# The rounded products read and write their 512 columns in pieces of 8, in turn from the two halves

## The chip, the cores and the metric

The kernel runs on one core of one Trainium2 chip. The metric is the device time of one execution in microseconds (us); the time before is the median of 3 runs.

## What is computed

The reference runs a chain of transformer layers in float32 on a sequence of 512 tokens of width 1024. The first block mixes four heads of a gated delta network with four heads of retention and follows with a convolutional gated MLP of width 2816. Two further layers, with a dilated window attention and a differential attention, each have an MLP of width 4096 with a squared ReLU. Norms stand between them. By far the most arithmetic is in the dense projections:

```python
proj = jnp.einsum('bsd,dc->bsc', n, w_in[l])
...
hdn = jnp.einsum('bsd,df->bsf', x, w_up)
...
return jnp.einsum('bsf,fd->bsd', jax.nn.silu(g) * u, w_down)
...
qkv = xn @ w_qkv
...
h = jax.nn.relu(xn @ w_in)
return (h * h) @ w_out
```

## The kernel before, in words

Activations lie transposed: a tile has 128 features on the partitions and all 512 tokens as its columns, so every projection is a sum over 128-row tiles of "weights (128 x 128, stationary) times activations (128 x 512, moving)" into one PSUM bank of 128 x 512 float32.

TensorE is fed with rounded float32 (`F32R`). To keep the accuracy, each operand is split into a rounded high part and a rounded rest: the activations into `n_hi` and `n_lo` (or `ff_hi` and `ff_lo`, `b_parts`), the weights into `w_hi` and `w_lo`. A product is then three matmuls into the same bank, high x high, high x low and low x high, lines 839, 840 and 841 of the helper `products`. Every dense projection of every layer goes through this helper. Other matmuls (transposes, attention scores and values, column sums) have lines of their own. Most take plain float32 operands; the helper for the scores of the second attention (L1477) and two lines for small gates (L1505, L1506, with 16 and 8 weight columns) use rounded ones but do not go through `products`.

Weights come in units of 256 output columns by 1024 rows (1 MB): SP issues the DMA into `raw`, ScalarE rounds it into `w_hi` (L1569, `split_hi`), VectorE computes `w_lo = raw - w_hi` (L1574, `split_lo`), and TensorE does the unit's 48 matmuls: 2 tiles of 128 output columns, 8 tiles of the sum, 3 matmuls each. `raw`, `w_hi` and `w_lo` have two buffers each. ScalarE waits for `w_used`, which TensorE counts up at the end of a unit, before it overwrites a buffer; TensorE waits for `lo_ready`. The results go to `proj_bank`, four banks in two groups of two; ScalarE or VectorE reads a bank once its last product has signalled, and signals `bank_free`.

The order of the work on TensorE is written out by hand: `project` runs over the units, and in the two attention layers a table of steps puts the attention's matmuls between the products (`layer_a_tensor`, `layer_b_tensor`). In SBUF two small unused tensors, `pad` (384 bytes a partition) at the front and `moving_pad` (160 bytes) ahead of the activations, set where the later tensors start. A tile of activations is 2048 bytes a partition, and the columns 0 to 255 of it are its first 1024 bytes.

Of the kernel before, what the change touches and what calls it, by code (L numbers as in the profile page):

```python
# [203 lines left out]
def build(nc, t, out):  # L204
# [7 lines left out]
    def sb(name, shape, dt=F32):  # L212
        return ctx.enter_context(nc.sbuf_tensor(name, shape, dt))
# [6 lines left out]
    with ctx:  # L220
# [4 lines left out]
        w_hi = sb("w_hi", [P, 2, UNIT], F32R)  # L225
        w_lo = sb("w_lo", [P, 2, UNIT], F32R)
# [606 lines left out]
            norm_pool(pool, 7)  # L833


        def products(b, j, tile, k, hi, lo, start, final):

            cols = slice(k * GC + tile * P, k * GC + tile * P + P)
            nc.tensor.matmul(b[:, :], w_hi[:, j % 2, cols], hi, start=start, stop=False)  # L839
            nc.tensor.matmul(b[:, :], w_hi[:, j % 2, cols], lo, start=False, stop=False)  # L840
            return nc.tensor.matmul(b[:, :], w_lo[:, j % 2, cols], hi, start=False, stop=final)  # L841

        def project(pe, ph, hi, lo, tiles_ready=None, norm=None, pairs_ready=None, order=range(KD), between=None, begun=0):

# [3 lines left out]
            def three(j, g, tile, k, src, start, final):  # L848
                return products(proj_bank[2 * g + tile], j, tile, k, hi[src], lo[src], start, final)
# [351 lines left out]
        def output(pe, ph, unit, k, hi, lo, ready):  # L1201

            if k == 0:
                pe.wait_ge(bank_free, ph.g0 + unit + 1)
                pe.wait_ge(lo_ready, ph.u0 + unit + 1)
            pe.wait_ge(ready[0], ready[1] + k + 1)
            for tile in range(2):
                ins = products(proj_bank[2 * unit + tile], unit, tile, k, hi[k], lo[k], k == 0, k == KD - 1)
                if k == KD - 1:
                    ins.then_inc(w_used if tile else tile0_ready, 1)  # L1210
# [26 lines left out]
        def layer_a_tensor(pe):  # L1237

            ph = p_qkvs[0]
            for step in range(A_STEPS):  # L1240
                u, tile, k = step // (2 * KD), step // KD % 2, step % KD
                attention_a_parts(pe, step)
                if step % (2 * KD) == 0:
                    pe.wait_ge(lo_ready, ph.u0 + u + 1)
                if u == 0:
                    k, tile = divmod(step, 2)
                    if step == 0:
                        pe.wait_ge(bank_free, ph.g0 + 1)
                    if tile == 0:
                        pe.wait_ge(norm_lo, KD * SPLIT[2] + k + 1)  # L1250
                elif k == 0:
                    if u <= 2:
                        pe.wait_ge(bank_free, ph.g0 + u + 1)
                    elif tile == 0:
                        pe.wait_ge(at("a_tile0"), u)
                    else:
                        pe.wait_ge(bank_free, ph.g0 + u + 2)
                ins = products(proj_bank[2 * (u == 1) + tile], u, tile, k, N_HI[k], N_LO[k], k == 0, k == KD - 1)
                if k == KD - 1:
                    ins.then_inc(w_used if tile else tile0_ready, 1)  # L1260
                if u == 1 and (tile, k) == (0, 7):
                    two_sums_of(pe)
                elif u == 1 and (tile, k) == (1, 1):
                    norm_spread(pe, 2)
# [1673 lines left out]
```

## Time and profile before

| what | value |
|---|---|
| median of 3 runs | 1899.64 us (1899.3 to 1900.44) |
| the profiled execution, its own time | 1901.63 us |
| its span, first to last instruction | 1899.8 us |
| mean granted TensorE clock | 0.997 of full speed |
| TensorE matmuls busy | 1880.5 us (99%), 9573 instructions |
| weight loads busy (they overlap the matmuls) | 1523.8 us (80%) |
| VectorE, ScalarE, GpSimd busy | 1052.5 us (55%), 770.4 us (41%), 78.6 us (4%) |

The profiled execution is 2.0 us longer than the median, and 1.8 us of it lie outside the span. Matmuls are pipelined, so one lasts longer in the profile (about 390 ns) than the time until the next starts; the time per matmul is read from the distances between starts or ends, not from its duration. A float32 matmul that is not rounded stands in the profile as two rows of instructions, each with a weight load of its own.

### The profile page before, as it was taken

How to read it: one execution, taken by the hardware profiler on the slowest of the kernel's cores; microseconds unless marked ns; L12 is line 12 of the kernel's file. 1: busy time of each engine (PE TensorE's matmuls, PEld its weight loads, DVE VectorE, ACT ScalarE, POOL GpSimd, SP SyncE). 2: the span in 40 equal slices, each digit the busy share in tenths (PEclk: the TensorE clock that was granted, in tenths of full speed). 3: DMA queues.
4: the chain of work that ended last, by engine and by line, in shares of the span. 5: the costliest groups of instructions: out<-in, count | busy, mean ns of one | idle time of the engine just before them, and what ended most of it. 6: DMA issues, size and time to landing. Idle time of an engine off the chain costs nothing.

```text
span 1899.8 us, 25523 instructions
## 1 busy us (share of the span) xinstructions
PE 1880.5 (99%) x9573; PEld 1523.8 (80%) x9573; DVE 1052.5 (55%) x1458; ACT 770.4 (41%) x967; POOL 78.6 (4%) x77
## 2 busy tenths in 40 slices
PE   8999999999999999999999999999999999999998
PEld 6778888888888788878888888887676788888887
DVE  7746855677367676566543244247778554323423
ACT  5472343555234344454432133136556543212412
POOL 0010001000000010000100000020000010000001
PEclk9999999999999999999999999999999999999999
DMA  6223122232332252212322322342322133223231
GB/s 238 89 87 116 47 68 67 89 103 73 111 108 83 70 158 83 89 53 83 106 93 89 111 89 92 107 130 86 106 84 87 36 99 110 89 93 106 88 103 53
DMA packets 146483, 178.92 MB, mean 94 GB/s; under 512 B 3549, under 2 KB 140381, under 8 KB 143968
## 3 DMA queue, kind: packets, MB, share of 16 engines
q1 hardware_dynamic: 143008, 160.44, 25.9%
q0 software_dynamic: 3104, 17.10, 2.8%
q8 instruction: 54, 0.88, 0.2%
q10 hardware_dynamic: 288, 0.26, 0.0%
q14 instruction: 29, 0.24, 0.0%
HBM read 173.48 MB, written 2.20 MB: 92 GB/s over the span
## 4 chain that ended last, share of the span: by engine, by line
PE 93%; DVE 4%; ACT 1%; issue 1%; DMA 0%; DVEq 0%; ACTq 0%
PE bank L839 28%; PE bank L841 27%; PE bank L840 27%; PE bank L960 2%; PE bank L1495 2%; PE bank L1477 1%; DVE w_lo L1574 1%; PE bank L966 1%; PE bank L1296 1%; PE bank L954 1%; ACT w_hi L1569 1%; PE bank L1349 1%; PE bank L1053 0%; PE bank L1018 0%; PE bank L1061 0%
## 5 line engine op out<-in xcount | busy, mean ns | idle before, releaser
L839 PE MATMUL bank<-n_hi,w_hi 128*128 128x512 f32 x1504 | 605.3, 402 | 7.6 <-DVE w_lo L1590 6.7
L1569 ACT ACTIVATE w_hi<-raw 128x2048 fp32r<-128x2048 f32 x152 | 291.4, 1917 | 732.2 <-PE bank L841 730.0
L841 PE MATMUL bank<-n_hi,w_lo 128*128 128x512 f32 x1504 | 587.5, 391 | 0.0
L840 PE MATMUL bank<-n_lo,w_hi 128*128 128x512 f32 x1504 | 587.4, 391 | 0.0
L1574 DVE TENSOR_TENSOR w_lo<-raw,w_hi 128x2048 fp32r<-128x2048 f32 x152 | 349.2, 2298 | 275.3 <-ACT w_hi L1569 273.4
L839 PEld LDWEIGHTS bank<-n_hi,w_hi 128*128 128x128 f32 x1504 | 283.3, 188 | 77.8 <-issue 20.7
L841 PEld LDWEIGHTS bank<-n_hi,w_lo 128*128 128x128 f32 x1504 | 283.3, 188 | 60.1
L840 PEld LDWEIGHTS bank<-n_lo,w_hi 128*128 128x128 f32 x1504 | 283.6, 189 | 59.7 <-issue 5.0
L840 PE MATMUL bank<-ff_lo,w_hi 128*128 128x512 f32 x848 | 330.0, 389 | 0.0
L839 PE MATMUL bank<-ff_hi,w_hi 128*128 128x512 f32 x784 | 306.0, 390 | 1.3 <-DVE w_lo L1574 1.3
L841 PE MATMUL bank<-ff_hi,w_lo 128*128 128x512 f32 x784 | 305.1, 389 | 0.0
L840 PEld LDWEIGHTS bank<-ff_lo,w_hi 128*128 128x128 f32 x848 | 159.2, 188 | 33.0 <-issue 0.5
L839 PEld LDWEIGHTS bank<-ff_hi,w_hi 128*128 128x128 f32 x784 | 147.2, 188 | 32.5 <-DVE w_lo L1574 1.7
L841 PEld LDWEIGHTS bank<-ff_hi,w_lo 128*128 128x128 f32 x784 | 147.2, 188 | 30.9
L2523 DVE SCALAR_TENSOR_TENSOR scratch<-bank,rstd 128x512 f32<-128x512 f32 x64 | 44.3, 692 | 133.5 <-PE bank L841 124.8
L2508 DVE TENSOR_TENSOR hT<-hT,bank 128x512 f32<-128x512 f32 (+1 forms) x70 | 48.1, 687 | 125.9 <-PE bank L841 123.1
L2290 DVE SCALAR_TENSOR_TENSOR scratch<-scratch,ffn_w 128x511 f32<-128x511 f32 x88 | 66.1, 751 | 16.8 <-DVE scratch L2290 6.0
L2164 ACT ACTIVATE scratch<-scratch,b_small 128x512 f32<-128x512 f32 x64 | 46.3, 724 | 39.8 <-DVE b_small L2763 38.4
L2760 DVE CUSTOM_DVE_ANT_0 scratch<-bank,b_bias 128x512 f32<-128x512 f32 x64 | 44.3, 691 | 23.4 <-PE bank L1477 19.3
L778 POOL TENSOR_TENSOR scratch<-scratch 128x1024 f32<-128x1024 f32 x5 | 13.5, 2709 | 977.0 <-ACT scratch L1667 977.0
L2278 DVE TENSOR_TENSOR scratch<-bank,rstd 128x512 f32<-128x512 f32 x44 | 30.4, 692 | 24.2 <-PE bank L841 16.8
L2530 DVE TENSOR_TENSOR ff_lo<-scratch,ff_hi 128x1024 f32 x32 | 39.2, 1226 | 8.1 <-ACT ff_hi L2037 7.6
(347 smaller groups left out, 1564.2 us busy)
## 6 DMA issues: line engine op xcount, KB each, us to landing
raw<-in_mlp_w_in SPq DMA_DIRECT2D x32, 1024.0 KB, 5.3
raw<-in_mlp_w_out SPq DMA_DIRECT2D x32, 1024.0 KB, 4.9
raw<-in_w_up SPq DMA_DIRECT2D x22, 1024.0 KB, 4.9
raw<-in_w_units SPq DMA_DIRECT2D x14, 1024.0 KB, 4.8
raw<-in_a_w_qkv SPq DMA_DIRECT2D x12, 1024.0 KB, 5.0
raw<-in_b_w_qkv SPq DMA_DIRECT2D x12, 1024.0 KB, 5.0
b_bias<-bias_table POOLq DMA_DIRECT2D x16, 448.0 KB, 4.4
raw<-in_w_down SPq DMA_DIRECT2D x8, 768.0 KB, 4.5
```

What stands on the lines that cost most here:

```text
L839: nc.tensor.matmul(b[:, :], w_hi[:, j % 2, cols], hi, start=start, stop=False)
L840: nc.tensor.matmul(b[:, :], w_hi[:, j % 2, cols], lo, start=False, stop=False)
L841: return nc.tensor.matmul(b[:, :], w_lo[:, j % 2, cols], hi, start=False, stop=final)
L960: ins = nc.tensor.transpose(b[:, i * P:(i + 1) * P], src(i), ident)
L1569: act.activation(w_hi[:, s, :], raw[:, s, :], ACT.Copy).then_inc(hi_ready, 1)
L1574: dve.tensor_tensor(w_lo[:, s, :], raw[:, s, :], w_hi[:, s, :].bitcast(F32), ALU.subtract).then_inc(lo_ready, 1)
L2164: done(act, act.activation(e, e, ACT.Exp, bias=b_small[:, 8 + 2 * (n % 4) + j:9 + 2 * (n % 4) + j], accum_out=b_small[:, 16 + 2 * (n % 4) ...
L2290: ins = dve.scalar_tensor_tensor(y, taken[:, n, 0:SEQ - back], w, y, ALU.mult, ALU.add)
L2508: ins = dve.tensor_tensor(h, h, b[:, :].unsqueeze(1), ALU.add)
L2523: ins = dve.scalar_tensor_tensor(scratch[:, 2 * g + tile, :], b[:, :], 0.0, rstd[:, :], ALU.max, ALU.mult)
L2530: done(dve, dve.tensor_tensor(ff_lo[:, bass.ds(it * 4 + 2 * g, 2), :], scratch[:, 2 * g:2 * g + 2, :], ff_hi[:, bass.ds(it * 4 + 2 * g, 2) ...
L2760: ring_done(dve, dve.tensor_tensor_reduce(b_s[:, n % 4, j, :], b[:, :], b_bias[:, h % 2, j, i * P:i * P + SEQ], 1.0, -FAR, ALU.add, ALU.ma ...
```

## The change

```diff
+        def woven(at_cols):
+            return at_cols.rearrange("p (h l e) -> p l h e", h=2, e=8)
+
         def products(b, j, tile, k, hi, lo, start, final):
 
             cols = slice(k * GC + tile * P, k * GC + tile * P + P)
-            nc.tensor.matmul(b[:, :], w_hi[:, j % 2, cols], hi, start=start, stop=False)
-            nc.tensor.matmul(b[:, :], w_hi[:, j % 2, cols], lo, start=False, stop=False)
-            return nc.tensor.matmul(b[:, :], w_lo[:, j % 2, cols], hi, start=False, stop=final)
+            out, hi, lo = woven(b[:, :]), woven(hi), woven(lo)
+            nc.tensor.matmul(out, w_hi[:, j % 2, cols], hi, start=start, stop=False)
+            nc.tensor.matmul(out, w_hi[:, j % 2, cols], lo, start=False, stop=False)
+            return nc.tensor.matmul(out, w_lo[:, j % 2, cols], hi, start=False, stop=final)
```

`woven` is another way of walking over the same 512 columns: 8 columns from column 0, 8 from column 256, 8 from column 8, 8 from column 264, and so on, 64 pieces in all, each 32 bytes long, with 1024 bytes between neighbours. The moving operand and the PSUM bank are both walked in this way, so each result lands in the column where it was before. The stationary operand, the number of matmuls, their order on TensorE and every wait stay as they are, and no instruction of another engine changes. In the built program a product's shape reads 128x32x2x8 where it read 128x512. The three lines become 843, 844 and 845.

## Rows read from the trace of the kernel before

**Rows 1.** The page: busy times, granted clock by slice, and the chain that ended last
```profile
PE 1880.5 (99%) x9573; PEld 1523.8 (80%) x9573; DVE 1052.5 (55%) x1458; ACT 770.4 (41%) x967; POOL 78.6 (4%) x77
...
PEclk9999999999999999999999999999999999999999
...
PE 93%; DVE 4%; ACT 1%; issue 1%; DMA 0%; DVEq 0%; ACTq 0%
PE bank L839 28%; PE bank L841 27%; PE bank L840 27%; PE bank L960 2%; PE bank L1495 2%; PE bank L1477 1%; DVE w_lo L1574 1%; PE bank L966 1%; PE bank L1296 1%; PE bank L954 1%; ACT w_hi L1569 1%; PE bank L1349 1%; PE bank L1053 0%; PE bank L1018 0%; PE bank L1061 0%
```

**Rows 2.** One line, L839: duration in ns minimum/median/maximum, first and last start, forms
```profile
L839 PE MATMUL bank<-n_hi,w_hi x1504: 387/389/802, 6.7 to 1800.1; 128*128 128x512 f32 x188
...
L839 PE MATMUL bank<-ff_hi,w_hi x784: 387/389/504, 283.6 to 1887.1; 128*128 128x512 f32 x196
...
L839 PE MATMUL bank<-b_parts,w_hi x64: 389/389/795, 1477.5 to 1537.6; 128*128 128x512 f32 x64
...
L839 PE MATMUL bank<-ff_lo,w_hi x32: 389/389/389, 298.2 to 330.2; 128*128 128x512 f32 x32
```

**Rows 3.** The chain in order of time, 1050 to 1060 us: start, length, what
```profile
1050.24 0.23 PE bank L839
1050.47 0.23 PE bank L840
1050.69 0.23 PE bank L841
...
1059.76 0.23 PE bank L839
```

**Rows 4.** Stretches: us, then busy (x instructions) of PE, PEld, DVE, ACT, POOL; clock, DMA
```profile
400.00:500.00 100.00, 100.00 (x443) 82.84 (x442) 68.09 (x71) 47.47 (x43) 0.00 (x0) 1.00 0.28 87
...
1000.00:1100.00 100.00, 100.00 (x443) 82.84 (x442) 30.77 (x23) 19.55 (x12) 0.00 (x0) 1.00 0.30 96
1000.00:1200.00 200.00, 200.00 (x884) 165.68 (x883) 71.59 (x55) 53.82 (x37) 0.00 (x0) 1.00 0.31 99
```

**Rows 5.** The chain, 134.5 to 138.1 us: eight rows of unrounded matmuls on 512 columns
```profile
134.57 3.43 PE bank L987 x8
```

**Rows 6.** The chain, 254.3 to 257.3 us: rows of 512, 384, 256, 128 columns, two each
```profile
254.71 2.16 PE bank L1061 x8
```

**Rows 7.** The chain, 76.6 to 80.7 us: rounded matmuls with 16 and 8 weight columns
```profile
76.99 0.23 PE bank L1505
77.23 0.23 PE bank L1506
...
80.69 0.53 PE bank L1514
```

**Rows 8.** Groups by line: the preparation of the weights, and what each waits for
```profile
L1569 ACT ACTIVATE w_hi<-raw 128x2048 fp32r<-128x2048 f32 x152 | 291.4, 1917 | 732.2 <-PE bank L841 730.0 <-ACT ff_hi L2024 0.6 <-ACT r_cols L1695 0.5
...
L1574 DVE TENSOR_TENSOR w_lo<-raw,w_hi 128x2048 fp32r<-128x2048 f32 x152 | 349.2, 2298 | 275.3 <-ACT w_hi L1569 273.4
```

**Rows 9.** DMA issues: tile and source, KB each, median us to landing
```profile
raw<-in_mlp_w_in SPq DMA_DIRECT2D x32, 1024.0 KB, 5.3
```

**Rows 10.** Stretches of the two attention layers, L839 alone: busy (x instructions) of PE, PEld
```profile
700.00:900.00 200.00, 89.75 (x221) 41.46 (x220) 0.99 0.27 85
1300.00:1500.00 200.00, 76.87 (x164) 30.69 (x163) 1.00 0.26 83
```

**Rows 11.** The chain: 16 matmuls of L1349, columns side by side, then every fourth column
```profile
743.97 1.02 PE bank L1349 x16
...
874.98 1.02 PE bank L1349 x16
```

## The prediction, made before the changed kernel ran

> **What bounds the kernel now.** I read the page first. TensorE has 1880.5 us of work in a span of 1899.8, and the chain that ended last is 93% TensorE; 82% of it lies on the three lines that the change touches [rows 1]. The granted clock is 9 in every slice, so nearly all of it runs at the full 2.4 GHz. The change must therefore be judged by one number: the time from one product to the next.
>
> How many products: L839 has 1504 + 784 + 64 + 32 = 2384 matmuls [rows 2], and each is followed by one of L840 and one of L841, so 3 x 2384 = 7152.
>
> How long each takes: in the chain by time, L839 ends the piece at 1050.24 us and again at 1059.76, with 42 pieces from the one to the other [rows 3]: 9.52 us / 42 = 226.7 ns. The counts agree: the second 100 us of 1000 to 1200 us add 884 - 443 = 441 rows [rows 4], 226.8 ns each. 7152 x 226.7 ns = 1621 us.
>
> How long it would have to take: 512 columns at one column per cycle of 2.4 GHz are 213.3 ns. Each product so pays **13.3 ns on top**, 7152 x 13.3 = 95 us in all. Two things about this surcharge can be read. It does not come from the other engines: 400 to 500 us have VectorE busy for 68 us and ScalarE for 47, 1000 to 1100 us have 31 and 20, and TensorE gets 443 rows into either [rows 4]. And it isn't paid by every matmul. Unrounded matmuls pass over their columns twice per row of the profile: eight rows of L987 on 512 columns take 3.43 us [rows 5], 428.8 ns each, where two passes are 426.7: 2.1 ns on top. Eight rows of L1061 with 2 x (512 + 384 + 256 + 128) columns take 2.16 us [rows 6]; their columns need 2.133 us, so 3.3 ns on top of each. These rows take in columns at half the rate at which the rounded products do. The surcharge therefore belongs to rounded matmuls, that is, either to the rate at which they fetch (or write) 4-byte columns, or to their start. Nor does it hang on the size of the weight load: the 16 matmuls with 16 and 8 weight columns take from 76.99 to 80.69 us, 231 ns each [rows 7], no less than the products with 128.
>
> **The change, part by part.** It removes and adds no instruction; it moves none; no wait is added. What it changes is the order of addresses in 7152 matmuls, on the read side and on the write side, and the cost or gain of that is not in the trace of before, since no rounded matmul there walks in pieces. I bound it from both sides.
>
> The gain. If the 13.3 ns are a stall that comes from reading (or writing) on through neighbouring addresses at the full rate, turning between two places 1024 bytes apart can take it away. The nearest rows are the unrounded ones, with 2.1 and 3.3 ns [rows 5, 6]; I take their middle, 2.7 ns. A product then takes 213.3 + 2.7 = 216.0 ns, 10.7 less: 7152 x 10.7 = 76.5 us. Nothing left on top at all would be 7152 x 13.3 = 95 us; that is the bound. At the other end a quarter of the stall might go, 3.3 ns or 24 us.
>
> The Trainium skill, "TensorE: Matmul & The Clock Gate", section "Back-to-back issue gap", gives the isolated gap as N/2.4 + 2.5 ns; for 512 columns that is 215.8 ns, and this case's rounded products, at 226.7, do not keep to it while the unrounded rows nearly do. By that figure the estimated gain would be 78 us.
>
> The loss. If each turn from one half to the other costs the time of one column, 213.3 / 512 = 0.417 ns, the 63 turns of a product cost 26.2 ns: 7152 x 26.2 = 188 us. Two columns' time each is 375 us, the other bound. The nearest row for another walk is on the write side: 16 matmuls of L1349 that write 128 columns side by side take 1.02 us, and 16 that write every fourth column take 1.02 us too [rows 11]. So a walk with jumps costs nothing there; but those are unrounded and take columns at half the rate. I take zero for the turns, by this row, and keep the bound for the range.
>
> The Trainium skill, "PSUM — Partial Sum Buffer", section "Specifications (TRN2)", says that any access pattern that isn't contiguous slows matmuls significantly; the rows of L1349, at 1.02 us both ways, don't show it, and the rule gives no figure from which the sum could be changed.
>
> What else could come to bound it. With products at 216 ns a unit of 48 lasts 10.4 us instead of 10.9. ScalarE's rounding (1.92 us) and VectorE's rest (2.30 us) come one after the other when TensorE lets go of a buffer, 4.2 us in all, and both sit idle before it: 730 us of ScalarE's idle time are spent waiting for L841 [rows 8]. A unit's DMA lands 5.3 us after its issue [rows 9]. Neither comes near 10.4. In the attention layers products also cover the softmax work, and there a shorter product may turn into a wait. L839 has 221 matmuls in 700 to 900 us and 164 in 1300 to 1500 [rows 10], so 3 x 385 = 1155 products; I let half of them give nothing: 578 x 10.7 = 6 us lost.
>
> The sum against the profiled execution: 1901.6 - 76.5 + 6 = 1831 us. It is 2.0 us longer than the median of the runs, so against that 1829; I say **1830**.
>
> **The rivals.**
>
> *The surcharge stays, and the turns are free: 1900 us.* The 13.3 ns may belong to the start of a rounded matmul: at the full rate nothing can be fetched ahead while the one before still reads, and each start then shows a few cycles of latency whatever the addresses. For it: the surcharge is the same in every calm stretch, to the tenth of a ns, and there is one width of rounded product only, so nothing in the trace tells "per start" from "per column". The matmuls with narrow weights, at 231 ns, keep it as well. Against it: the unrounded rows start just as often and lose 2.1 to 3.3 ns. The time is 1899.6 within 2. The Trainium skill, "Vector Engine (DVE) Microarchitecture Reference", section "Measured stream behaviour on trn2", has jumps between runs of two or more neighbouring words free on VectorE; if TensorE's reads were alike, the change would do nothing unless the stall hangs on the addresses.
>
> *Each turn costs: 2087 us.* A fetch at the full rate has no spare time, as the 13.3 ns suggest; a jump to another address then loses a slot. One slot of a column per turn gives 226.7 + 26.2 = 252.9 ns a product and 1899.6 + 188 = 2087. The mechanism decides early: with the whole stall gone, a turn that costs over 10.7 / 63 = 0.17 ns makes the kernel slower. For it: 63 turns against one run, at a rate twice that of any row that shows free jumps. Against it: L1349 [rows 11], and that each piece is 8 whole columns.
>
> *The change doesn't do what it says.* If the walk were cut into several instructions there would be more than 7152 rows; the built program has as many matmuls as before, in the same order, so I give this no chance of its own.
>
> **How the numbers follow.** The surcharge goes, all or in part: 0.44; its own range is 1804 (1899.6 - 95) to 1876 (a quarter goes). Nothing happens: 0.27. Turns cost: 0.29, of which I put about half at up to one column's time per turn. The predicted time is that of the likeliest case, 1830. The range goes from 1804 to 2087: 0.44 + 0.27 + 0.14 = 0.85, less a little at the edges. Cases of both signs hold most of the chance, hence its width. A difference over 0.2% (3.8 us) can be told from no change; the chances are faster 0.44, same 0.27, slower 0.29.
>
> **What would show each step.** Right: 7152 matmuls on the three new lines; some 463 rows in 100 us where 441 were; pieces of the chain near 216 ns in calm stretches, the same for all three lines; L987, L1061 and L1477 as long as before; VectorE waits somewhat more visible in the attention layers. The first rival: 226.7 ns again. The second: pieces of 250 ns or more, and the weight loads' idle time grown by as much. Wrong in the step on cover: products at 216 ns but under 60 us gained, with waits for VectorE's L1574 or the softmax in the chain. A surcharge that shrinks by a part only would mean that the stall is counted by addresses, of which the walk avoids some.

## The result, and the profile after

The changed kernel takes 2009.86 us (median of 4 runs, 2008.71 to 2013.28) against 1899.74 before: a ratio of **1.0582**, with a 95% interval of 1.0564 to 1.0601. It lost 110 us where I had forecast a gain of 70. The sign is that of the rival "each turn costs", whose time was 2087.

The page of the changed kernel has the same instructions, the same clock and the same work on the other engines as before [rows 1]; only TensorE's busy time grew, and its share of the chain with it, from 93% to 97%:

```profile
PE 1996.8 (99%) x9573; PEld 1540.3 (77%) x9573; DVE 1052.1 (52%) x1458; ACT 770.2 (38%) x967; POOL 80.4 (4%) x77
...
PEclk9999989999999999999999999999999999999999
...
PE 97%; DVE 1%; ACT 1%; issue 0%; DMA 0%; DVEq 0%; ACTq 0%
PE bank L843 29%; PE bank L844 28%; PE bank L845 28%; PE bank L964 3%; PE bank L1499 1%; PE bank L1481 1%; PE bank L970 1%; PE bank L958 1%; PE bank L1300 1%; PE bank L1353 1%; DVE w_lo L1578 0%; PE bank L1022 0%; PE bank L1057 0%; PE bank L1065 0%; PE bank L991 0%; ACT w_hi L1573 0%
```

The loss lies in the time from one product to the next. The stretches 1000 to 1100 and 1000 to 1200 us of the changed kernel (columns as in [rows 4]) differ by 824 - 413 = 411 rows of TensorE, 243.3 ns each, where 441 stood before:

```profile
1000.00:1100.00 100.00, 100.00 (x413) 77.88 (x412) 35.24 (x28) 29.13 (x21) 0.00 (x0) 1.00 0.29 93
1000.00:1200.00 200.00, 200.00 (x824) 155.75 (x823) 68.52 (x53) 51.63 (x35) 0.00 (x0) 1.00 0.28 92
```

The chain in order of time agrees; each piece is one product, to be held against [rows 3]:

```profile
1050.15 0.24 PE bank L844
1050.39 0.25 PE bank L845
1050.63 0.24 PE bank L843
...
1058.91 0.24 PE bank L844
```

From 1050.15 to 1058.91 us are 36 pieces: 8.76 / 36 = 243.3 ns, 16.7 more than before and 30.0 more than 512 columns need. The matmuls outside the helper kept their time: the eight rows of the unrounded L991 (L987 before) take 3.43 us and those of L1065 (L1061 before) 2.16, as in [rows 5, 6].

```profile
141.29 3.43 PE bank L991 x8
...
265.84 2.16 PE bank L1065 x8
```

7152 products x 16.7 ns would be 119 us, and the span grew by 2011.5 - 1899.8 = 111.7. Part of the difference was taken out of TensorE's waits: its idle time fell from 19.3 us (1899.8 - 1880.5) to 14.7 (2011.5 - 1996.8). The rest, about 3 us, was not followed further.

The matmul's duration in the profile can stand in for the distance, and it can be had for a single line. L844 with `n_lo` lasts 404/407/628 ns (minimum/median/maximum) where a straight product lasts about 389 [rows 2]: about 18 more, where the distance grew by 16.7. It is the rougher gauge: with one and the same walk the three lines of a product can differ by over 10 ns, so where a walk is judged by durations all three count, and differences of a few ns say nothing.

```profile
L844 PE MATMUL bank<-n_lo,w_hi x1504: 404/407/628, 7.2 to 1905.1; 128*128 128x512 f32 x188
```

### The profile page after: what moved, and what is told of

The parts are those of the page before. It is cut to its first block, busy times and chain, and to the rows that moved or that the text cites. A ratio compares the mean times of both kernels' runs of the same rounds, so it can differ in the third digit from the quotient of the medians.

```text
span 2011.5 us, 25523 instructions
## 1 busy us (share of the span) xinstructions
PE 1996.8 (99%) x9573; PEld 1540.3 (77%) x9573; DVE 1052.1 (52%) x1458; ACT 770.2 (38%) x967; POOL 80.4 (4%) x77
## 4 chain that ended last, share of the span: by engine, by line
PE 97%; DVE 1%; ACT 1%; issue 0%; DMA 0%; DVEq 0%; ACTq 0%
PE bank L843 29%; PE bank L844 28%; PE bank L845 28%; PE bank L964 3%; PE bank L1499 1%; PE bank L1481 1%; PE bank L970 1%; PE bank L958 1%; PE bank L1300 1%; PE bank L1353 1%; DVE w_lo L1578 0%; PE bank L1022 0%; PE bank L1057 0%; PE bank L1065 0%; PE bank L991 0%; ACT w_hi L1573 0%
## 5 line engine op out<-in xcount | busy, mean ns | idle before, releaser
L843 PE MATMUL bank<-n_hi,w_hi 128*128 128x512 f32 x1504 | 628.7, 418 | 6.8 <-DVE w_lo L1594 6.6
L844 PE MATMUL bank<-n_lo,w_hi 128*128 128x512 f32 x1504 | 611.5, 407 | 0.0
L845 PE MATMUL bank<-n_hi,w_lo 128*128 128x512 f32 x1504 | 611.4, 407 | 0.0
L844 PEld LDWEIGHTS bank<-n_lo,w_hi 128*128 128x128 f32 x1504 | 285.9, 190 | 79.5 <-issue 5.1
L844 PE MATMUL bank<-ff_lo,w_hi 128*128 128x512 f32 x848 | 344.2, 406 | 0.0
L843 PE MATMUL bank<-ff_hi,w_hi 128*128 128x512 f32 x784 | 320.0, 408 | 0.4 <-DVE w_lo L1578 0.4
L845 PE MATMUL bank<-ff_hi,w_lo 128*128 128x512 f32 x784 | 319.0, 407 | 0.0
L844 PEld LDWEIGHTS bank<-ff_lo,w_hi 128*128 128x128 f32 x848 | 160.8, 190 | 45.2 <-issue 0.5
```

The source lines that it names most:

```text
L843: nc.tensor.matmul(out, w_hi[:, j % 2, cols], hi, start=start, stop=False)
L844: nc.tensor.matmul(out, w_hi[:, j % 2, cols], lo, start=False, stop=False)
L845: return nc.tensor.matmul(out, w_lo[:, j % 2, cols], hi, start=False, stop=final)
```

## The experiments

Two questions stood first. Does the price lie where the moving operand is read or where the bank is written? And is the straight walk's surcharge of 13.3 ns one per start or one per column?

**Read side alone, write side alone.** In the first, only the moving operand is woven; the results then land in other columns than the reference's, and the same goes for the second:

```diff
-            out, hi, lo = woven(b[:, :]), woven(hi), woven(lo)
+            out, hi, lo = b[:, :].rearrange("p (l h e) -> p l h e", h=2, e=8), woven(hi), woven(lo)
```

> The moving operand alone is walked in pieces of 8; the bank is written straight on, so the columns of each dense product land in another order than the reference's. The changed kernel has 243.3 ns from one product to the next (584 cycles of 2.4 GHz), the kernel before 226.7 ns (544). Theory R, the price of the turns is paid on the read side in SBUF: 243.3 ns here and about 2010 us. Theory W, it is paid where PSUM is written: 226.7 ns here and 1900 us. If both sides pay a part, something between. If the two sides hamper each other only when they differ, more than 243.3.

In the second, only the bank:

```diff
-            out, hi, lo = woven(b[:, :]), woven(hi), woven(lo)
+            out = woven(b[:, :])
+            hi, lo = (v.rearrange("p (l h e) -> p l h e", h=2, e=8) for v in (hi, lo))
```

> The bank alone is walked in pieces of 8; the moving operand is read straight on, so the columns of each dense product land in another order than the reference's. Theory R (the turns are paid on the read side): 226.7 ns from one product to the next and 1900 us. Theory W (on the write side): 243.3 ns and 2010 us.

Read side alone: 2011.06 us, ratio 1.0589 (1.0558 to 1.0619). Write side alone: 1900.27 us, ratio 0.9999 (0.9988 to 1.0011). The same stretches, first of the kernel with the woven read, then of the one with the woven write:

```profile
1000.00:1100.00 100.00, 100.00 (x412) 77.87 (x412) 34.96 (x28) 29.39 (x21) 0.00 (x0) 1.00 0.29 93
1000.00:1200.00 200.00, 200.00 (x823) 155.75 (x823) 68.23 (x53) 51.63 (x35) 0.00 (x0) 1.00 0.29 92
```

```profile
1000.00:1100.00 100.00, 100.00 (x443) 82.81 (x442) 29.05 (x21) 19.38 (x11) 0.00 (x0) 1.00 0.31 101
1000.00:1200.00 200.00, 200.00 (x884) 165.62 (x883) 69.97 (x54) 53.65 (x36) 0.00 (x0) 1.00 0.31 99
```

That is 411 rows in 100 us, exactly the change's number, against 441, exactly that of before. The whole price is paid where the moving operand is read from SBUF. Writing the bank in pieces of 8 at the full rate is free, which goes against the rule of the Trainium skill, "PSUM — Partial Sum Buffer", section "Specifications (TRN2)", that a pattern that isn't contiguous slows matmuls; 32-byte pieces at least don't.

**Longer pieces, shorter products.** The change with pieces of 32 columns (`e=32`):

> Both sides walked in pieces of 32 columns, 15 turns a product where the changed kernel has 63. Theory T, each turn has a price of its own: 63 turns cost 16.7 ns, 0.265 ns each, so 15 cost 4.0 ns: 230.6 ns and about 1928 us. Theory B, the walk meets the stationary operand's reads in the same part of SBUF more often, however long the pieces are: it stays near 243 ns and 2010 us. Theory S, long pieces take some of the 13.3 ns of stall away that the straight walk has: below 226.7 ns.

1962.55 us, ratio 1.0333 (1.0303 to 1.0363); 847 - 425 = 422 rows in the second 100 us, 237.0 ns. With 15 turns in place of 63 the surcharge over the straight walk fell from 16.7 to 10 ns, not to 4. One fixed price for every turn is out.

```profile
1000.00:1100.00 100.00, 100.00 (x425) 79.87 (x423) 33.12 (x24) 25.72 (x17) 0.00 (x0) 1.00 0.27 89
1000.00:1200.00 200.00, 200.00 (x847) 159.80 (x846) 71.57 (x55) 55.68 (x38) 0.00 (x0) 1.00 0.28 89
```

The kernel before with shorter corrections, whose last columns are left out; its two narrow lines (L1505, L1506) are walked in pieces of 8 on both sides, by an edit of their own that is not shown:

```diff
-            nc.tensor.matmul(b[:, :], w_hi[:, j % 2, cols], lo, start=False, stop=False)
-            return nc.tensor.matmul(b[:, :], w_lo[:, j % 2, cols], hi, start=False, stop=final)
+            nc.tensor.matmul(b[:, 0:384], w_hi[:, j % 2, cols], lo[:, 0:384], start=False, stop=False)
+            return nc.tensor.matmul(b[:, 0:256], w_lo[:, j % 2, cols], hi[:, 0:256], start=False, stop=final)
```

> The kernel before, with the high x low product of each three cut to the first 384 columns and the low x high product to the first 256; the corrections of the other columns are left out. The 16 narrow products of the gates are walked in pieces of 8. Is the surcharge of the straight walk paid per start or per column? Per start (13.3 ns each): 384 columns take 173.3 ns, 256 take 120.0. Per column (one in sixteen): 170.0 and 113.3 ns. If it came from meeting the 128 reads of the next weight load: both rows keep 13.3 ns, or more, since the load fills more of the shorter one. The narrow products (16 and 8 weight columns): 231 ns on average as before if the turns cost only against a wide weight load, about 248 ns if each turn has its own price. Time about 1900 - 2384 x (0.0533 + 0.1067) = 1519 us, the attention's waits on top.

1642.46 us, ratio 0.8648 (0.8605 to 0.8690), not 1519: L839 now has to wait for VectorE's `w_lo`, since a unit no longer lasts long enough to cover it. The question is answered in a stretch without such waits, at a granted clock of 1.00. The chain in order of time:

```profile
1000.04 0.23 PE bank L839
1000.27 0.17 PE bank L840
1000.44 0.12 PE bank L841
...
1009.56 0.23 PE bank L839
```

From 1000.04 to 1009.56 us are 18 times three products: 9.52 / 18 = 528.9 ns for three, whose 1152 columns need 480.0. That leaves 48.9 ns on top of the three, 16.3 each. A price of 13.3 ns per start would give 520.0 ns, one column in sixteen 510.0. So the surcharge did not shrink with the columns, it grew; and it is no fixed 13.3 ns either. By the ends of the pieces the product of 512 columns pays about 20 ns, that of 384 about 14 and that of 256 about 15. The durations, as groups of lines (columns as in the page's part 5), are less clear:

```profile
L840 PE MATMUL bank<-n_lo,w_hi 128*128 128x384 f32 x1504 | 510.6, 339 | 0.0
L841 PE MATMUL bank<-n_hi,w_lo 128*128 128x256 f32 x1504 | 428.6, 285 | 0.0
...
L839 PE MATMUL bank<-ff_hi,w_hi 128*128 128x512 f32 x784 | 314.6, 401 | 14.9 <-DVE w_lo L1574 10.1 <-DVE ff_lo L2301 4.7 <-DVE ff_lo L2664 0.2
```

384 columns need 160.0 ns and 256 need 106.7, so 179 and 178 ns remain beside the columns, against 389 - 213.3 = 176 for the 512 columns of before [rows 2]. But these are means, which a few long products pull up; the medians are 394, 337 and 281 ns, and what remains beside the columns is 181, 177 and 174, some 3 ns less for each 128 columns, as a price per column would have it. The distances decide, since they are what the products cost: the surcharge of the three is 48.9 ns where a price per column leaves 30.0, so it isn't counted by columns. Whether it belongs to the start as such or to the weight load that comes with every start, the third theory of the expectation ("13.3 ns, or more"), this run does not tell, and a surcharge that grew fits the latter at least as well. And the narrow products, with 16 and 8 weight columns, woven by 8:

```profile
L1505 PE MATMUL bank<-n_hi,ab_both x8: 404/404/405, 70.5 to 73.9; 128*16 128x512 f32 x8
L1506 PE MATMUL bank<-n_lo,ab_both x8: 404/407/408, 70.7 to 74.1; 128*8 128x512 f32 x8
```

404 to 407 ns, the durations of the change's wide products (404 to 409), and their starts, 70.49 to 74.14 us for 15 steps, lie 243.3 ns apart as there. The woven read takes the same time whatever the size of the weight load beside it. The expectation had 231 or about 248: these products took 231 ns walked straight [rows 7], so the walk costs them 12 ns and not 16.7.

**Many walks at once.** Each of the 8 tiles of the sum got a walk and lines of its own. One of the eight blocks:

```diff
+            if k == 6:
+                out, hi, lo = (walk(v, 4, 8) for v in (b[:, :], hi, lo))
+                nc.tensor.matmul(out, wh, hi, start=start, stop=False)
+                nc.tensor.matmul(out, wh, lo, start=False, stop=False)
+                return nc.tensor.matmul(out, wl, hi, start=False, stop=final)
```

> Eight walks in one kernel, one for each of the 8 tiles of the sum, so that three matmuls in a row share a walk and each walk has lines of its own. Written as parts x piece: straight; 2 x 2; 2 x 4; 2 x 16; 2 x 64; 2 x 128; 4 x 8; 8 x 8 (2 x 8 is the change; 4 x 8 takes 8 columns from each quarter in turn, with 512 bytes between). Known: straight 226.7 ns, 2 x 8 243.3, 2 x 32 236.7. Theory N, the price grows with the number of turns: 2 x 128 (3 turns) about 227 to 229, 2 x 64 (7 turns) 230 to 233, 2 x 16 (31 turns) between 237 and 243, 2 x 4 and 2 x 2 (127 and 255 turns) over 250; 4 x 8 and 8 x 8 at 243 like 2 x 8, having as many turns. Theory D, the price hangs on the distance, since a turn comes back to a place at a multiple of 1024 bytes: 4 x 8 (512 bytes) and 8 x 8 (256 bytes) cost clearly less or more than 243.3. Theory P, pieces below 16 or 32 bytes are what costs: 2 x 4 and 2 x 2 far over 243, the long pieces all near 236.

> Eight more walks: 16 x 8 (128 bytes between the pieces), 32 x 8 (64 bytes), 32 x 4 (64 bytes, 16-byte pieces), 128 x 2 (16 bytes, 8-byte pieces), 4 x 32, 16 x 16, straight backwards, and 2 x 8 again as a yardstick (243.3 ns). Theory N (number of turns alone): 16 x 8 and 32 x 8 at 243, 4 x 32 at 236.7, 16 x 16 as 2 x 16, backwards 226.7. Theory D (distance): some of the short distances fall to 226.7 or below, since they step on to neighbouring places; 128 x 2 reads each stretch of 16 bytes twice and costs most if stretches are what is fetched.

The middle line of six of the blocks (name, count, then ns minimum/median/maximum). First kernel: straight, 2 x 2, 2 x 4, 2 x 16, 2 x 64 and 4 x 8:

```profile
L846 PE MATMUL bank<-n_lo,w_hi x188: 387/389/628, 7.3 to 1930.3; 128*128 128x512 f32 x188
...
L851 PE MATMUL bank<-n_lo,w_hi x188: 500/509/627, 9.9 to 1931.1; 128*128 128x512 f32 x188
...
L856 PE MATMUL bank<-n_lo,w_hi x188: 411/422/427, 12.3 to 1932.1; 128*128 128x512 f32 x188
...
L861 PE MATMUL bank<-n_lo,w_hi x188: 402/402/407, 13.8 to 1932.8; 128*128 128x512 f32 x188
...
L866 PE MATMUL bank<-n_lo,w_hi x188: 387/387/398, 15.2 to 1933.5; 128*128 128x512 f32 x188
...
L876 PE MATMUL bank<-n_lo,w_hi x188: 389/392/394, 18.0 to 1934.9; 128*128 128x512 f32 x188
```

Second kernel: 16 x 8, 32 x 4 (here all three lines), 128 x 2, backwards, and 2 x 8 as a yardstick:

```profile
L846 PE MATMUL bank<-n_lo,w_hi x188: 380/382/628, 7.2 to 2030.2; 128*128 128x512 f32 x188
...
L855 PE MATMUL bank<-n_hi,w_hi x188: 380/391/787, 11.2 to 2031.3; 128*128 128x512 f32 x188
L856 PE MATMUL bank<-n_lo,w_hi x188: 379/382/399, 11.4 to 2031.5; 128*128 128x512 f32 x188
L857 PE MATMUL bank<-n_hi,w_lo x188: 379/394/399, 11.7 to 2031.8; 128*128 128x512 f32 x188
...
L861 PE MATMUL bank<-n_lo,w_hi x188: 629/647/652, 13.0 to 2032.4; 128*128 128x512 f32 x188
...
L876 PE MATMUL bank<-n_lo,w_hi x188: 395/402/402, 18.4 to 2035.0; 128*128 128x512 f32 x188
...
L881 PE MATMUL bank<-n_lo,w_hi x188: 404/406/409, 19.8 to 2035.8; 128*128 128x512 f32 x188
```

Against 389 for straight and 406 for 2 x 8: pieces of 8 bytes are ruinous (509, and 647 for 128 x 2, which reads each 16 bytes in two visits and takes 230 to 262 ns more by the line); from 16 bytes on, the number of turns is no guide. 32 x 4 has 127 turns and medians of 391, 382 and 394 on its three lines, on average those of the straight walk; 2 x 4 has 127 too and 417, 422 and 416; straight but backwards, with no turn at all, 395, 402 and 396. The five walks not shown (2 x 128, 8 x 8, 32 x 8, 4 x 32 and 16 x 16) fit no rule of turns either: on the middle line 8 x 8, with 63 turns, has 393, and 4 x 32, with 15, has 402. The two kernels took 2045.44 and 2150.86 us (one run each). These are walks among neighbours with other walks; each candidate had to be run alone.

**Walks of their own.** Three kernels with one walk each (`h=4, e=8`; `h=16, e=8`; `h=32, e=4`):

> All products in pieces of 8 taken in turn from the four quarters: 63 turns as in the change, but 512 bytes between neighbours instead of 1024, and a step back of 1536. Theory D (what costs is the distance, a multiple of 1024 bytes): 230 to 233 ns as in the sweep, about 1930 to 1945 us. Theory N (number of turns): 243.3 ns and 2010 us.

> All products in pieces of 8 with 128 bytes between neighbours, taken from sixteen parts: 63 turns again. In the sweep its three lines took 225.9, 225.3 and 229.9 ns. Theory D: 222 to 230 ns, 1870 to 1925 us, possibly below the kernel before. Theory N: 243.3 ns and 2010 us.

> All products in pieces of 4 columns (16 bytes) with 64 bytes between neighbours, taken from thirty-two parts: 127 turns, twice those of the change. In the sweep 228.2, 222.6 and 229.6 ns. Theory D: 221 to 230 ns, 1860 to 1925 us, possibly the version that beats both. Theory N: over 255 ns and over 2090 us.

4 x 8: 1926.11 us, ratio 1.0136 (1.0116 to 1.0157); 867 - 434 = 433 rows in the second 100 us, 230.9 ns. 16 x 8: 1904.54, ratio 1.0026 (0.9999 to 1.0053), with nine of its ten runs from 1890 to 1918. 32 x 4: 1893.08, ratio **0.9966 (0.9951 to 0.9981)**. The number of turns is refuted again: 63, 63 and 127. The stretches of 16 x 8 show something else:

```profile
400.00:500.00 100.00, 100.00 (x457) 85.19 (x456) 65.05 (x67) 45.69 (x40) 0.00 (x0) 1.00 0.27 85
400.00:600.00 200.00, 200.00 (x911) 170.41 (x910) 128.79 (x134) 81.96 (x73) 0.00 (x0) 1.00 0.30 97
1000.00:1100.00 100.00, 100.00 (x435) 81.70 (x434) 29.44 (x21) 19.37 (x11) 0.00 (x0) 1.00 0.30 95
1000.00:1200.00 200.00, 200.00 (x868) 163.39 (x867) 69.03 (x52) 51.48 (x34) 0.00 (x0) 1.00 0.30 96
```

911 - 457 = 454 rows in 100 us are 220.3 ns a product, 868 - 435 = 433 are 230.9: the same lines at the same clock, in two rhythms, each held for whole stretches. It isn't the operand: between 330 and 600 us L844 has a median of 382 ns with `n_lo` and with `ff_lo`, between 1500 and 1700 us 391 with both. The quicker rhythm leaves 7 ns beside the 512 columns, where the straight walk has 13.3: a walk can take half of the surcharge away. 32 x 4 has two as well, 223.2 ns (898 - 450 = 448 rows) from 500 to 600 us and 226.8 (884 - 443 = 441) from 1100 to 1200.

```profile
400.00:500.00 100.00, 100.00 (x450) 83.86 (x449) 64.64 (x68) 45.71 (x40) 0.00 (x0) 1.00 0.27 90
400.00:600.00 200.00, 200.00 (x898) 167.73 (x897) 126.39 (x132) 81.57 (x73) 0.00 (x0) 1.00 0.30 97
1000.00:1100.00 100.00, 100.00 (x443) 82.79 (x442) 30.84 (x21) 21.33 (x13) 0.00 (x0) 1.00 0.29 95
1000.00:1200.00 200.00, 200.00 (x884) 165.59 (x883) 72.44 (x54) 53.60 (x36) 0.00 (x0) 1.00 0.30 95
```

**Where the tiles start.** The kernel before, without `moving_pad`, and with one of 168 columns in place of 40:

```diff
-        sb("moving_pad", [P, 40])
+        pass
```

```diff
-        sb("moving_pad", [P, 40])
+        sb("moving_pad", [P, 168])
```

> The kernel before without its small tensor ahead of the activations: the moving tiles start 160 bytes earlier, at 96 bytes past a multiple of 256. If the straight walk's 13.3 ns are a price per start or per column, they stay: 226.7 ns and 1900 us. If they come from where the stretches of addresses begin (a theory under which the walk's turns cost for the same reason), a product takes a different time, by 0.8 ns or more, 6 us of the kernel.

> The kernel before with the moving tiles 512 bytes later, so that they start at the same place modulo 1024 as the weights. Theory A, the moving reads meet the weight loads: the time per product changes. Theory I, the moving read is slowed by itself alone (the narrow weight loads were as slow as the wide ones): 226.7 ns and 1900 us as before.

Without the pad: 1939.99 us, ratio 1.0209 (1.0192 to 1.0226), 859 - 431 = 428 rows in 100 us, 233.6 ns. With 512 bytes more: 1900.10 us, ratio 1.0000 (0.9991 to 1.0010). So the straight walk's time does hang on an address, but not on 512 bytes more or less. The first of the two:

```profile
1000.00:1100.00 100.00, 100.00 (x431) 80.43 (x430) 31.90 (x23) 23.63 (x15) 0.00 (x0) 1.00 0.28 92
1000.00:1200.00 200.00, 200.00 (x859) 160.91 (x858) 72.86 (x56) 55.76 (x38) 0.00 (x0) 1.00 0.29 92
```

Is it the tile's own start, or its place against the weights? The next kernel takes 160 bytes off the front, so that both move:

```diff
-        sb("pad", [P, 96])
+        sb("pad", [P, 56])
```

> The kernel before with its first small tensor 160 bytes shorter, so that the weights and the moving tiles all start 160 bytes earlier. The moving tiles then lie as far off a multiple of 256 as without the second small tensor (1940 us, 231 to 237 ns a product), but at the old distance from the weights. Theory A (what counts is where the moving reads lie against the weight loads): 226.7 ns and 1900 us. Theory I (what counts is where the moving tile itself starts): 231 ns or more and 1925 to 1940 us.

1900.22 us, ratio 1.0000 (0.9989 to 1.0011), 884 - 443 = 441 rows. The moving tiles start where they started in the slow kernel, and nothing is lost. What counts for the straight walk is where the moving operand lies against what lies ahead of it in SBUF; of that, TensorE reads the weights in these products, so a meeting of the two reads is the nearest reading, which no run shows by itself. And the change with its tiles 64 bytes later:

```diff
-        sb("moving_pad", [P, 40])
+        sb("moving_pad", [P, 56])
```

> The change with the moving tiles 64 bytes later. Theory I (the walk is slowed by its own reads alone, and a tile's start matters by its first stretch): 243.3 ns within 2 and 2010 us within 10. Theory A (against the weight loads): another time per product, several ns off, since 64 bytes move the one stream against the other by 16 columns.

2009.08 us (one run), 824 - 413 = 411 rows, 243.3 ns: the woven walk doesn't feel these 64 bytes, nor, as the narrow products showed, the size of the weight load. The 160 bytes that slow the straight walk were not tried on it, nor the 64 on the straight one.

**Distance.** First by leaving columns out. The walk of the change over 480 columns, between halves of 240:

```diff
+            nc.tensor.matmul(b[:, :], w_hi[:, j % 2, cols], hi, start=start, stop=False)
+            nc.tensor.matmul(woven(b[:, 0:480]), w_hi[:, j % 2, cols], woven(lo[:, 0:480]), start=False, stop=False)
+            return nc.tensor.matmul(woven(b[:, 0:480]), w_lo[:, j % 2, cols], woven(hi[:, 0:480]), start=False, stop=final)
```

(The four lines of the change that these replace are not shown.)

> High x high straight on 512 columns; high x low and low x high cut to the first 480 columns (the corrections of the last 32 are left out) and walked 2 x 8 between halves of 240 columns, so that neighbouring pieces lie 960 bytes apart, 64 short of 1024. 480 columns need 200.0 ns. Theory D in its strict form (a turn comes back to the same place modulo 1024, or modulo a smaller power of two over 64): the cost of the turns falls, 212 to 219 ns a product. Theory H (each hop over some hundred bytes costs, wherever it lands): about 200 + 30 x 60/64 = 228 ns, as in the change.

1903.19 us (one run), 880 - 441 = 439 rows in 100 us, 227.8 ns as the mean of one product of 512 columns and two of 480. If the straight one had kept 226.7, the other two took 228.3 each, where 228 were foretold for hops at any distance and 212 to 219 for the strict form of theory D. Then with the distance as the only variable, one block for each:

```diff
+        def two_runs(v, d):
+            return bass.AP(tensor=v.tensor, offset=v.offset, ap=[v.ap[0], [8, 32], [-d // 4, 2], [1, 8]])
```

> One walk, one variable. For products with n_hi, tiles 1 to 7 of the sum read two runs of 256 columns in turn, 8 columns at a time (63 turns), the second run lying D bytes before the first; D is 64, 128, 256, 512, 768, 896 and 1024 for tiles 1 to 7. The bank is written straight on; the second run reads other columns than the reference's, so the sums are other sums. Tile 0 and the products without n_hi are read straight. Theory M, the cost comes with certain distances (multiples of a power of two): 64 and 128 cheap (222 to 230 ns), 512 and 1024 dear, 1024 at 243. Theory H, each turn has one price whatever the distance: all seven at 243. Theory G, it grows with the distance: 64 cheapest, then steadily up to 243 at 1024.

> The same with D = 1088, 1152, 1280, 2048, 4096, 8192 and 1536 bytes for tiles 1 to 7. Theory M: 2048, 4096 and 8192 as dear as 1024 (243 ns) or dearer, 1088 and 1152 as cheap as 64 and 128. Theory H: all at 243. Theory G: all above 243, 8192 most.

First kernel, straight and then D = 64, 128, 256 and 1024 bytes; second kernel, D = 1088 and 8192 (its L876):

```profile
L846 PE MATMUL bank<-n_lo,w_hi x188: 387/389/628, 7.4 to 1851.9; 128*128 128x512 f32 x188
...
L851 PE MATMUL bank<-n_lo,w_hi x188: 402/406/628, 10.0 to 1852.6; 128*128 128x512 f32 x188
...
L856 PE MATMUL bank<-n_lo,w_hi x188: 402/404/409, 12.0 to 1853.3; 128*128 128x512 f32 x188
...
L861 PE MATMUL bank<-n_lo,w_hi x188: 404/409/409, 13.5 to 1854.1; 128*128 128x512 f32 x188
...
L881 PE MATMUL bank<-n_lo,w_hi x188: 404/407/409, 19.3 to 1857.0; 128*128 128x512 f32 x188
```

```profile
L851 PE MATMUL bank<-n_lo,w_hi x188: 402/403/628, 9.8 to 1852.6; 128*128 128x512 f32 x188
...
L876 PE MATMUL bank<-n_lo,w_hi x188: 404/406/409, 17.6 to 1856.2; 128*128 128x512 f32 x188
```

The medians of all fourteen distances, on all three lines of each, lie between 403 and 409 ns (the kernels took 1958.32 and 1958.37 us, one run each). For a walk between two runs in pieces of 8 the distance is all but indifferent, from 64 bytes to 8192: theory H is right for this walk, and M and G fall.

**Two more candidates**, with short pieces and few turns back (`h=64, e=4` and `h=16, e=4`):

> Pieces of 4 columns (16 bytes) with 32 bytes between neighbours: every second stretch of 16 bytes, then the others; 127 turns, of which one goes back. 32 x 4 (127 turns, three back) took 223.3 or 226.7 ns by the stretch and 1893 us. If turns back are what costs in the change (31 of them), this is at or below 32 x 4: 220 to 227 ns, 1850 to 1900 us. If the number of turns counts: over 255 ns.

> Pieces of 4 columns with 128 bytes between neighbours: 127 turns, seven back. If turns back are what costs: a little over 32 x 4, 225 to 232 ns, 1890 to 1940 us. If the number of turns counts: over 255 ns. If only the times of the pieces against the weight loads count: another of the values that are 3.33 ns apart (220.0, 223.3, 226.7, 230.0), which cannot be foretold.

1930.02 us, ratio 1.0156 (1.0139 to 1.0172), and 2031.33, ratio 1.0687 (1.0669 to 1.0705); in the second 100 us after 1000 us 867 - 435 = 432 rows, 231.5 ns, and 813 - 407 = 406 rows, 246.3 ns, none of the four values that the last theory named. Turns back are no guide either: one of them costs more than three (32 x 4), and seven cost more than the change's 31.

## Why the prediction was wrong

**What bounds the kernel** was read rightly: TensorE alone, one number, 7152 products at 226.7 ns, and no other engine in the way. The changed kernel's loss is that number's, 243.3.

**"The gain. If the 13.3 ns are a stall that comes from reading on through neighbouring addresses ... turning between two places can take it away."** This is the first step that failed. I put 76.5 us to this term, and no product of the changed kernel got shorter. The shorter products show that the surcharge isn't counted by columns: with a quarter of the columns gone it was 16.3 ns a product instead of 13.3. In that the first rival was nearer. I gave the rival 0.27 and the stall 0.44 on the strength of the unrounded rows, which start as often and lose 2.1 to 3.3 ns. That comparison showed only that not every matmul pays the surcharge. It said nothing of what it hangs on. Nor was the rival right that addresses don't matter: moving the tiles against the weights by 160 bytes made the surcharge 20 ns, and the walk 16 x 8, in its quicker rhythm, 7. A walk can lower it, then; this one does not, and by what rule is open.

**"I take zero for the turns, by this row" (L1349).** The second failure, and the costlier one. The row walks with jumps on the write side. The write side is indeed free, at the full rate too. But the change turns on the read side as well, which cost 16.7 ns a product where the sum had zero, and none of the rows taken for it has a read that turns. The row answered for half of the change, and I let it stand for the whole. It was misread besides: its 16 pieces are rows, two for each of 8 unrounded matmuls on 128 columns, and at two passes each they would need 16 x 106.7 ns = 1.71 us, where they took 1.02; so the row does not show "half the rate" either. That the measured time lies within the stated range is no merit of the working: the range was so wide because it also held losses, and the time was forecast on the side of the gain.

**The rival "each turn costs"** had the sign, but not the law or the size: 16.7 ns over the straight walk for 63 turns, 0.26 ns each, where it took 0.417. With 15 turns it is 10 ns, and 32 x 4 has 127 turns and none of the cost. That its 2087 us came within 4% of the time is luck. So "0.26 ns a turn" is a quotient, not a price.

**What else could bound it, and that the change does what it says** came out as written: 9573 matmuls before and after, L991 and L1065 unchanged, no wait in place of another.

**What stays open.** Why two runs in pieces of 8 cost 16.7 ns at any distance, four runs only about 4, thirty-two runs in pieces of 4 nothing and sixteen such runs 20, was not settled. The number of turns, of turns back and, for two runs, the distance are each ruled out as the one cause; so are, for the woven walk, the size of the weight load and 64 bytes of the tile's place. Where the reads of a product lie in time against those of the next weights was varied only through addresses. It could differ from walk to walk, and the two rhythms of 16 x 8 speak for something of the kind; that is argued, not shown.

## What to carry to other kernels

Before a row is taken as the price of a changed access pattern, check that it has the pattern on the same side (read or write) and at the same rate: a free pattern on one side says nothing of the other. In a kernel bound by back-to-back rounded matmuls, read the moving operand straight on. Where it can't be, avoid pieces of 8 bytes, which cost over 100 ns a product here, and measure the others, since pieces of 16 bytes cost anything from nothing to some 30 ns. Treat the places of moving tiles and weights as something to measure: 160 bytes were worth 40 us here. A surcharge that is constant to the tenth of a nanosecond invites a story; cut the instruction short first, to see whether it is one per start or one per column.

## What the runs showed of the hardware that was not expected

- The write side of a matmul takes a walk in 32-byte pieces with 1024 bytes between them at the full rate at no cost: 1900.27 against 1899.7 us.
- Most times per product fall on steps. 220.0, 223.3, 226.7, 236.7 and 243.3 ns are 66, 67, 68, 71 and 73 times 3.33 ns, the time of 8 columns; the counts in 100 us (454, 448, 441, 422, 411) lie within one row of these; the bare 512 columns are 64 steps, 213.3 ns. The 428 rows without `moving_pad` and the 406 of 16 x 4 fit 70 and 74 steps. Not every walk keeps to one step: 4 x 8 and the slower rhythm of 16 x 8 have 433 rows, 230.9 ns, between two of them. That the time goes in such steps is read from these values alone.
- The same lines can run in two rhythms, 220 or 231 ns (16 x 8), for a hundred microseconds and more, at a granted clock of 1.00 in both. Nine of its ten runs scatter by 28 us where those of the kernel before scatter by 2.
- A straight walk backwards is slower than forwards (durations 395 to 402 against 389 ns), and one over pieces of 16 bytes with 64 between (32 x 4) is a little faster. With it the kernel takes 1893.08 us, ratio 0.9966 (0.9951 to 0.9981), below both kernels; the gain is 7 us, and I would not carry it over unmeasured.
